# Linear attention in a hybrid backbone: chunk sums, square sums and two conditioning blocks in another order and other banks

## The chip, the cores and the metric

The kernel runs on one core of one Trainium2 chip. The metric is the device time of one launch in microseconds (us), given as the median of some runs. The engines are TensorE (PE, matrix products, with PEld for its weight loads), VectorE (DVE), ScalarE (ACT), GpSimd (POOL) and SyncE (SP, which here issues the weight transfers).

## The reference, cut to what matters

Two layers of a diffusion backbone over 256 latent tokens and 256 context tokens, width 1024, all in float32. Layer 0 mixes tokens by a gated linear attention (GLA, 4 heads, chunks of 64 tokens, forward and backward) beside a convolution; layer 1 by attention. A mixture of 16 experts follows each. Every norm is modulated by rows computed from a conditioning vector. The GLA part, for one direction:

```python
q_t = qc * jnp.exp(cum); k_t = kc * jnp.exp(-cum); k_end = kc * jnp.exp(last - cum)
att = jnp.where(mask, jnp.einsum('bhnid,bhnjd->bhnij', q_t, k_t), 0.0)
o_intra = jnp.einsum('bhnij,bhnjv->bhniv', att, vc)
u = jnp.einsum('bhnjd,bhnjv->bhndv', k_end, vc).astype(jnp.float32)
def step(s, inp):
    dec, uu = inp
    return dec[..., None] * s + uu, s
o_inter = jnp.einsum('bhnid,bhndv->bhniv', q_t, s_prev)
```

The outputs of both directions are summed, normed over the 128 values of a head, multiplied by a gate, and go with the convolution's output through one output projection:

```python
o = rms_norm(o_f + flip(o_b)) * gla_norm_g
o = o.transpose(0, 2, 1, 3).reshape(b_, t_, GLA_HEADS * GLA_DV) * jax.nn.silu(r)
out = jnp.concatenate([o, u.astype(o.dtype)], axis=-1) @ w_out
```

The conditioning rows of a layer are six slices of one product:

```python
mod = (silu_c @ ada_w[l] + ada_b[l])[:, None, :]
sh1, sc1, g1, sh2, sc2, g2 = jnp.split(mod, 6, axis=-1)
```

## The kernel before, in words

Each engine runs its own list of instructions in the order in which the code writes them; semaphores order the engines against each other. Nothing is planned at run time.

The weights come in blocks of 2 MB. `weight_stream` (L119) lists them in order of use; `ring_places` (L137) gives each one of six slots of `ring`, and SP issues them in that order (`load`, L509), each once the block six places earlier has been used (`block_used`). A few blocks go beside the ring into `xh` or `gm`. The conditioning weights of layer 1 are twelve blocks, named `("ada", 1, 0)` to `("ada", 1, 11)`; `ada_block(g, n)` (L616) multiplies block n of group g, eight matmuls with 32 stationary columns into the four partition quarters of one bank of PSUM. Group 4 is the last group: its blocks 8 to 11 are needed only for layer 1's second norm. `ada_added(g)` (L1823) adds the finished bank to the bias row on DVE, and `mod_rows(g)` (L2594) lets POOL store the row.

The GLA part works on pairs of heads, pt = 0 and 1, and for each pair on both directions d. The steps on PE, in `gla` (L841), are these. `turn_keys(pt)` transposes the end-decayed keys (L847), and ACT copies them out (`keys_taken`, L1638). `scores(pt)` makes the attention scores in four banks. DVE masks and adds them (`masked`, L2387). `chunk_sums(pt, d)` makes the eight states that a direction adds, in two banks, one for even and one for odd chunks. `inside(pt, hh)` multiplies masked scores by values (L874). DVE runs the chain of states over the chunks (`recurrence`, L2409: two copies and twelve multiply-adds). `across(pt)` multiplies queries by states, 28 matmuls of 64 columns (L888). ACT takes the outputs (`outputs_taken`, L1644), PE sums their squares over the head by a matrix of ones (`square_sums`, L835), ACT takes roots (`output_roots`, L1654), DVE inverts and scales (`normed_outputs`, L2424), and `even_out` (L937) is the output projection, whose first half goes over the convolution's four chunks of channels before it comes to the heads' four (L948).

In PSUM's eight banks, pair 0 has its scores in 0 to 3 and its outputs in 0 and 2; pair 1 has its scores in 4 to 7 and its outputs in 4 and 6. The square sums of a pair go into its own output banks.

After the projection come norm, router (`rows_and_router`, L963) and experts. In `rows_and_router` PE waits for DVE's choice of experts (`chosen`, L1014), and again for the slots (L1035); the four blocks of group 4 are multiplied ahead of these two waits, two and two. POOL then gathers the rows of the first expert from memory, and PE transposes them (L1136).

Of the kernel before, what the change touches and what calls it, by code (L numbers as in the profile page):

```python
# [118 lines left out]
def weight_stream():  # L119
# [12 lines left out]
    tail = [("eout", 0, 0), ("eout", 0, 1)] + ada(1, 8, 9, 10, 11) + moe_blocks(0)  # L132
# [30 lines left out]
def hybrid_dit(nc, A, out):  # L163
# [4 lines left out]
    with ctx:  # L168
# [169 lines left out]
        KV_BANK = (((4, 5), (1, 3)), ((1, 3), (5, 7)))  # L338
# [113 lines left out]
        ADA_BANK = (6, 2, 3, 2, 5)  # L452
# [9 lines left out]
        def ada_last(g, h):  # L462
            l, a, n = ADA_GROUPS[g]
            return at["ada", l, 2 + h if g == 0 else 2 * (a + n) - 1]
# [147 lines left out]
        def _(pe):  # L612
# [3 lines left out]
            def ada_block(g, n):  # L616
# [6 lines left out]
                if g:  # L623
                    w, s, k = flat(i).rearrange("p (c n) -> p c n", c=2), n // 4, n % 4
                    for c in range(2):
                        for q in range(4):
                            m = nc.tensor.matmul(ps[32 * q:32 * q + 32, ADA_BANK[g], :],  # L627
                                                 silu_c[:, 2 * k + c, 10 - 2 * s:42 - 2 * s], w[:, c, 512 * q:512 * q + 512],
                                                 start=n == 0 and c == 0, stop=True, skip_group_check=True)
# [205 lines left out]
            def square_sums(heads):  # L835
                for h in heads:
                    pe.wait_ge(sem("o_taken"), h + 1)
                    mm(ps[:, O_BANK[h // 2][h % 2], :], ones, (qT if h % 2 == 0 else kT)[:, h // 2, :])\
                        .then_inc(sem("o_sumsq"), 1)

            def gla():  # L841
# [20 lines left out]
                def chunk_sums(pt, d):  # L862
                    for n in range(NCH):
# [6 lines left out]
                    m.then_inc(sem("kv_sum"), 1)  # L870
# [43 lines left out]
                pe.wait_ge(sem("ketok_ready"), 4)  # L914
                chunk_sums(1, 0)
# [3 lines left out]
                chunk_sums(1, 1)  # L919
                inside(1, 1)  # L920
                across(1)
# [15 lines left out]
            def even_out():  # L937
# [3 lines left out]
                pe.wait_ge(sem("o_root"), 2)  # L941
# [21 lines left out]
            def rows_and_router(l):  # L963
# [46 lines left out]
                if l == 0:  # L1010
                    pe.wait_ge(sem("h2_act"), 2)
                    ada_block(4, 0)
                    ada_block(4, 1)
# [11 lines left out]
                else:  # L1025
# [7 lines left out]
                    ada_block(4, 2)  # L1033
# [122 lines left out]
            def down(l, e, p, i, t):  # L1156
                pe.wait_ge(arrival(i), 16 * NTH[i] + 16 * t)
                pe.wait_ge(sem("hidT_ready"), EB[l] + e + 1)
                if l == 0 and isinstance(e, int) and e == 0:
                    pe.wait_ge(sem("ada_added"), 6)  # L1160
# [277 lines left out]
        def _(act):  # L1438
# [215 lines left out]
            def output_roots(pt):  # L1654
                for hh in range(2):
                    act.wait_ge(sem("o_sumsq"), 2 * pt + hh + 1)
                    A_((qT if hh == 0 else kT)[:, pt, :], ps[:, O_BANK[pt][hh], :], ACT.Sqrt, scale=1.0 / DV, bias=eps)\
# [7 lines left out]
            def even_mixer():  # L1665
# [1145 lines left out]
```

## Time and profile before

| | us |
|---|---|
| median of 3 runs | 1047.66 (1046.27 to 1048.7) |
| the profiled execution's own time | 1039.51 |
| its span, first to last instruction | 1037.7 |
| PE busy | 949.4 (91%) |
| DVE busy | 623.6 (60%) |
| mean granted TensorE clock | 0.967 of full |

Busy times are sums over an engine's instructions; PE's matmuls overlap in its pipeline, so its busy time says when it had work and not how fast it went. The granted clock of TensorE has two levels, full (1.00, 2.4 GHz) and half (0.50, 1.2 GHz); a window that covers both shows a mean. Each float32 matmul appears as two records, so a count in the trace is twice that of the code. Times in the sections below are from the start of the span.

### The profile page before, as it was taken

The page shows a single profiled execution, that of the slowest core. Times are in us where ns is not written, and L with a number is a line of the kernel's source. Part 1 is how long each engine was busy: PE and PEld are TensorE (multiplying, and loading weights), DVE is VectorE, ACT ScalarE, POOL GpSimd, SP SyncE. Part 2 cuts the span into 40 slices and gives each one's busy share as a digit, 9 for nine tenths or more (in the row PEclk, how much of TensorE's full clock was granted, in tenths as well). Part 3 has the DMA queues.
Part 4 walks back from the last instruction along what each step waited for, and adds up shares of the span by engine and source line. Part 5 has one row for each costly group of instructions (what it writes and reads, how often), then busy time and mean ns, then how long its engine had stood idle before and what let it go on. Part 6 is the DMA issues. An engine that isn't in the chain of part 4 may idle for free.

```text
span 1037.7 us, 19786 instructions
## 1 busy us (share of the span) xinstructions
PE 949.4 (91%) x7940; PEld 575.5 (55%) x7940; DVE 623.6 (60%) x1516; ACT 178.0 (17%) x339; POOL 114.9 (11%) x176
## 2 busy tenths in 40 slices
PE   3999999989998799999999997997997999988896
PEld 1443433457445588988988973443646455543442
DVE  1200799787456586676675636467435977775553
ACT  2100022353024010000000013225413000000001
POOL 7100100102300100000001132100101100000000
PEclk9999999997999699999999998999997999999999
DMA  9999876442826999999999959646034989999994
GB/s 332 398 392 369 327 268 218 164 163 84 250 91 243 383 357 362 403 417 405 391 402 407 424 181 356 245 167 237 6 104 180 346 339 400 399 385 412 417 429 171
DMA packets 51354, 311.94 MB, mean 301 GB/s; under 512 B 7096, under 2 KB 8888, under 8 KB 33632
## 3 DMA queue, kind: packets, MB, share of 16 engines
q1 hardware_dynamic: 36752, 277.88, 68.2%
q0 software_dynamic: 9376, 21.19, 6.7%
q10 hardware_dynamic: 5168, 12.06, 3.1%
q8 instruction: 41, 0.67, 0.3%
q14 instruction: 17, 0.14, 0.0%
HBM read 300.52 MB, written 17.25 MB: 306 GB/s over the span
## 4 chain that ended last, share of the span: by engine, by line
PE 69%; DMA 16%; DVE 9%; issue 2%; SPq 2%; ACT 2%; POOL 0%; ACTq 0%; DVEq 0%; POOLq 0%
PE ps L614 46%; PE ps L1054 9%; DMA ring<-in_moe_w_gate 8%; PE ps L948 3%; PE ps L627 3%; DMA ring<-in_moe_w_down 2%; DMA ring<-in_ada_w 2%; PE ps L1097 2%; PE ps L1175 2%; SPq L515 2%; DMA y_rows<-ar 1%; PE ps L888 1%; DMA xh<-y_rows,sm 1%; DMA ar<-h_rows,sm 1%; PE ps L1418 1%
## 5 line engine op out<-in xcount | busy, mean ns | idle before, releaser
L614 PE MATMUL ps<-ring,ar 128*32 128x384 f32 (+6 forms) x3872 | 479.8, 466 | 17.9 <-DMA ring<-in_moe_w_gate 13.7
L614 PEld LDWEIGHTS ps<-ring,ar 128*32 128x32 f32 (+2 forms) x3872 | 198.7, 121 | 145.3 <-issue 87.1
L1054 PE MATMUL ps<-ring,ar 128*32 128x128 f32 x1488 | 167.8, 275 | 0.0
L1054 PEld LDWEIGHTS ps<-ring,ar 128*32 128x32 f32 x1488 | 163.7, 111 | 2.7
L2171 DVE STREAM_TRANSPOSE ar<-ar 32x256 f32<-32x256 f32 x304 | 132.2, 435 | 5.0 <-issue 0.6
L614 PE MATMUL ps<-xh,ring 128*128 128x512 f32 x256 | 114.9, 603 | 0.7 <-DMA ring<-in_even_w_in 0.7
L2214 DVE TENSOR_TENSOR ar<-ar,ps 128x384 f32<-128x384 f32 (+2 forms) x33 | 15.9, 482 | 132.1 <-PE ps L1054 68.1
L614 PE MATMUL ps<-ring,xh 128*128 128x512 f32 x192 | 85.9, 604 | 1.9 <-ACT xh L1478 1.6
L614 PEld LDWEIGHTS ps<-xh,ring 128*128 128x128 f32 x256 | 48.3, 192 | 64.2 <-issue 62.9
L2343 DVE SCALAR_TENSOR_TENSOR ar<-ar,cpar 128x512 f32<-128x512 f32 x120 | 79.6, 742 | 0.0
L1530 ACT ACTIVATE ar<-ps 128x384 f32<-128x384 f32 (+2 forms) x33 | 14.3, 433 | 289.7 <-PE ps L614 205.7
L614 PEld LDWEIGHTS ps<-ring,xh 128*128 128x128 f32 x192 | 36.5, 193 | 48.6 <-issue 45.6
L2201 DVE STREAM_TRANSPOSE ar<-ar 32x64 f32<-32x64 f32 x256 | 60.5, 236 | 4.5
L2193 DVE STREAM_TRANSPOSE ar<-ar 32x128 f32<-32x128 f32 x144 | 59.5, 413 | 2.9
L1097 PE MATMUL ps<-ring,ar 128*32 128x256 f32 x256 | 57.9, 379 | 0.0
L2650 POOL COPY sm<-sm 96x1 int32 (+3 forms) x32 | 6.0, 187 | 342.4 <-DVE ar L2171 318.3
L627 PE MATMUL ps<-ring,silu_c 128*32 128x512 f32 x320 | 39.9, 619 | 0.0
L2311 DVE TENSOR_TENSOR ar<-ps,gm 128x512 f32<-128x512 f32 x12 | 8.3, 689 | 51.7 <-PE ps L614 39.8
L1097 PEld LDWEIGHTS ps<-ring,ar 128*32 128x32 f32 x256 | 28.0, 110 | 18.1
L614 PE MATMUL ps<-ar 128*128 128x512 f32 (+3 forms) x112 | 33.3, 464 | 4.6 <-ACT ar L1767 2.4
L1535 ACT ACTIVATE ar<-ps 128x512 f32<-128x512 f32 x16 | 9.6, 598 | 149.3 <-PE ps L614 149.3
L2654 POOL DMA_INDIRECT ar<-h_rows,sm x32 | 31.2, 976 | 27.9 <-POOL sm L2650 26.8
(371 smaller groups left out, 908.9 us busy)
## 6 DMA issues: line engine op xcount, KB each, us to landing
ring<-in_moe_w_gate SPq DMA_DIRECT2D x31, 2048.0 KB, 17.1
ring<-in_moe_w_up SPq DMA_DIRECT2D x30, 2048.0 KB, 15.6
ring<-in_moe_w_down SPq DMA_DIRECT2D x30, 2048.0 KB, 19.1
ring<-in_ada_w SPq DMA_DIRECT2D x24, 2048.0 KB, 10.5
ring<-in_even_w_in SPq DMA_DIRECT2D x5, 2048.0 KB, 14.0
y_rows<-ar POOLq DMA_DIRECT2D x17, 384.0 KB, 10.5
ring<-in_odd_w_in SPq DMA_DIRECT2D x3, 2048.0 KB, 18.1
y_rows<-ar ACTq DMA_DIRECT2D x16, 288.0 KB, 8.9
```

Source lines behind the costliest of these rows:

```text
L515: sp.dma_start(wide, s).then_inc(arrival(i), 16)
L614: return nc.tensor.matmul(o, l, r, start=start, stop=stop)
L627: m = nc.tensor.matmul(ps[32 * q:32 * q + 32, ADA_BANK[g], :], silu_c[:, 2 * k + c, 10 - 2 * s:42 - 2 * s], w[:, c, 512 * q:512 * q + 512] ...
L948: m = nc.tensor.matmul(ps[:, j, :], mix[:, c, j * P:(j + 1) * P], blk(i)[:, c, :], start=(c == 4), stop=(c == 3), skip_group_check=True)
L1054: m = nc.tensor.matmul(ps[96:128, bank, g * P:(g + 1) * P], xgT[:, p, c, 32 * g:32 * g + 32], w[:, c, 3 * P:HID], start=c == 0 and g == 0, ...
L1097: nc.tensor.matmul(ps[96:128, 5, 256 * g:256 * g + 256], tokens(g, c), w[:, c, 768:D], start=c == 0 and g == 0, stop=c == HC - 1 and g == ...
L1175: m = nc.tensor.matmul(acc(j, h), mixw[64 * h:64 * h + 64, p, j * P:(j + 1) * P], yb[64 * h:64 * h + 64, p, 0:512], start=False, stop=True ...
L2171: m = V.transpose(xgT[32 * q:32 * q + 32, p, :, slots], xg[slots, p, :].rearrange("s (c q i) -> s q c i", c=KC, q=4)[:, q, :, :])
L2193: V.transpose(hidT[32 * q:32 * q + 32, p, :, 32 * r:32 * r + 32], cols[:, q, :, :])
L2201: m = V.transpose(hidT[32 * q:32 * q + 32, p, 0:2, 32 * r:32 * r + 32], cols[:, q, :, :])
L2343: V.scalar_tensor_tensor(acc[n], u_in[:, n, :, bass.ds(t, 256)], cpar[:, n, bass.ds(t, 1)], acc[n], ALU.mult, ALU.add).then_inc(sem("conv_ ...
L2654: G.indirect_dma_start(xg[0:CAP[l], p, :], None, h2_rows, bass.IndirectOffsetOnAxis(ap=idxc[0:CAP[l], p:p + 1], axis=0), bounds_check=NT * ...
```

## The change

The tail of the weight stream is in another order: blocks 8 and 9 of layer 1's conditioning weights stand ahead of the output projection's two blocks, 10 and 11 behind them.

```diff
-    tail = [("eout", 0, 0), ("eout", 0, 1)] + ada(1, 8, 9, 10, 11) + moe_blocks(0)
+    tail = ada(1, 8, 9) + [("eout", 0, 0), ("eout", 0, 1)] + ada(1, 10, 11) + moe_blocks(0)
```

Banks: the backward chunk sums of pair 1 go into 0 and 2, and the square sums get banks of their own (`SQ_BANK`). Blocks 8 and 9 are summed in bank 6, 10 and 11 in bank 5.

```diff
-        KV_BANK = (((4, 5), (1, 3)), ((1, 3), (5, 7)))
+        KV_BANK, SQ_BANK = (((4, 5), (1, 3)), ((1, 3), (0, 2))), ((5, 7), (4, 6))
...
-        ADA_BANK = (6, 2, 3, 2, 5)
+        ADA_BANK = (6, 2, 3, 2, 6)
+        LATE_BANK = 5
```

PE's order in `gla`, where `chunk_sums` can now make some chunks only:

```diff
-                chunk_sums(0, 0)
+                chunk_sums(0, 0).then_inc(sem("kv_sum"), 1)
                 pe.wait_ge(sem("att_masked"), 2)
+                chunk_sums(0, 1, range(0, NCH, 2))
                 inside(0, 0)
                 pe.wait_ge(sem("att_masked"), 4)
-                chunk_sums(0, 1)
+                chunk_sums(0, 1, range(1, NCH, 2)).then_inc(sem("kv_sum"), 1)
                 inside(0, 1)
                 pe.wait_ge(sem("qk_exp"), 8)
                 pe.wait_ge(sem("ke_diff"), 4)
+                ada_block(4, 0)
+                ada_block(4, 1)
                 across(0)
                 turn_keys(1)
+                pe.wait_ge(sem("ada_added"), 6)
                 scores(1)
-                square_sums((0, 1))
                 pe.wait_ge(sem("ketok_ready"), 4)
-                chunk_sums(1, 0)
+                chunk_sums(1, 0).then_inc(sem("kv_sum"), 1)
+                pe.wait_ge(sem("o_taken"), 2)
+                chunk_sums(1, 1).then_inc(sem("kv_sum"), 1)
                 pe.wait_ge(sem("att_masked"), 6)
                 inside(1, 0)
                 pe.wait_ge(sem("att_masked"), 8)
-                chunk_sums(1, 1)
                 inside(1, 1)
+                square_sums((0, 1))
                 across(1)
```

In `even_out` the wait for pair 0's roots goes. In `rows_and_router` one block stands ahead of each of the two waits instead of two.

```diff
-                pe.wait_ge(sem("o_root"), 2)
...
                     pe.wait_ge(sem("h2_act"), 2)
-                    ada_block(4, 0)
-                    ada_block(4, 1)
+                    ada_block(4, 2)
...
                     pe.wait_ge(sem("h2_act"), NT)
-                    ada_block(4, 2)
                     ada_block(4, 3)
```

ACT copies pair 1's keys before it takes pair 0's outputs. DVE adds blocks 8 and 9 between `decayed(1)` and `masked(1)`, and 10 and 11 where the whole group was added before:

```diff
+                keys_taken(1)
                 outputs_taken(0)
-                keys_taken(1)
...
                 decayed(1)
+                ada_added(4)
                 masked(1)
...
+            def late_added():
+                dve.wait_ge(sem("block_used"), at["ada", 1, 11] + 1)
+                V.tensor_tensor(modrow_of(4), modrow_of(4), ps[:, LATE_BANK, :], ALU.add).then_inc(sem("ada_added"), 1)
...
-                    ada_added(4)
+                    late_added()
```

PE in the first head pair, before (`gm` holds this pair's queries and keys, `ar` the values and states; 64x128 is a chunk sum):

```order
L614 MATMUL ps<-gm 128x128 x16
L614 MATMUL ps<-ar,gm 64x128 x16
L874 MATMUL ps<-gm,ar 128x128 x4
L614 MATMUL ps<-ar,gm 64x128 x16
L874 MATMUL ps<-gm,ar 128x128 x4
L888 MATMUL ps<-gm,ar 128x64 x28
```

And PE at the same place now:

```order
L615 MATMUL ps<-gm 128x128 x16
L615 MATMUL ps<-ar,gm 64x128 x24
L876 MATMUL ps<-gm,ar 128x128 x4
L615 MATMUL ps<-ar,gm 64x128 x8
L876 MATMUL ps<-gm,ar 128x128 x4
L628 MATMUL ps<-ring,silu_c 32x512 x16
L890 MATMUL ps<-gm,ar 128x64 x28
```

Eight chunk sums moved ahead of the first `inside`, and the sixteen matmuls of two conditioning blocks stand ahead of `across(0)`.

PE in the second head pair, before (`xh` holds its queries and keys; `ar,cst 128x512` is a square sum):

```order
L847 MATMUL ps<-cst,xh 128x128 x8
L614 MATMUL ps<-xh 128x128 x16
L614 MATMUL ps<-ar,cst 128x512 x2
L614 MATMUL ps<-ar,xh 64x128 x16
L874 MATMUL ps<-xh,ar 128x128 x4
L614 MATMUL ps<-ar,xh 64x128 x16
L874 MATMUL ps<-xh,ar 128x128 x4
L888 MATMUL ps<-xh,ar 128x64 x28
```

And PE there now:

```order
L849 MATMUL ps<-cst,xh 128x128 x8
L615 MATMUL ps<-xh 128x128 x16
L615 MATMUL ps<-ar,xh 64x128 x32
L876 MATMUL ps<-xh,ar 128x128 x8
L615 MATMUL ps<-ar,cst 128x512 x2
L890 MATMUL ps<-xh,ar 128x64 x28
```

All 32 chunk sums now stand ahead of both `inside` steps, and the square sums of pair 0 behind them.

SP's transfers around the output projection's weights, before:

```order
L515 DMA ring<-in_even_w_in 128x8x512
L515 DMA ring<-in_even_w_out 128x8x512 x2
L515 DMA ring<-in_ada_w 128x2x2048 x4
L515 DMA ring<-in_moe_w_gate 128x4096
L515 DMA ring<-in_moe_w_up 128x4096
```

And SP there now:

```order
L516 DMA ring<-in_even_w_in 128x8x512
L516 DMA ring<-in_ada_w 128x2x2048 x2
L516 DMA ring<-in_even_w_out 128x8x512 x2
L516 DMA ring<-in_ada_w 128x2x2048 x2
L516 DMA ring<-in_moe_w_gate 128x4096
L516 DMA ring<-in_moe_w_up 128x4096
```

Two conditioning blocks moved ahead of the projection's two; the expert blocks behind them take the slots in this new order of release.

## Rows read from the trace of the kernel before

**Rows 1.** Timeline of PE (start, duration in us, line, tiles, records; idle before).

```profile
219.36 1.04 PE L847 MATMUL ps<-cst,gm 128*128 128x128 f32 x8
220.32 2.06 PE L614 MATMUL ps<-gm 64*128 64x128 f32 x32
...
226.06 1.10 PE L614 MATMUL ps<-ar,gm 64*64 64x128 f32 x32 [0.94 <-DVE gm L2406]
227.09 1.16 PE L874 MATMUL ps<-gm,ar 128*128 128x128 f32 x8
230.84 6.03 PE L888 MATMUL ps<-gm,ar 64*128 64x64 f32 x56 [2.59 <-DVE ar L2421]
236.80 1.97 PE L847 MATMUL ps<-cst,xh 128*128 128x128 f32 x8
...
241.92 1.98 PE L614 MATMUL ps<-ar,cst 128*128 128x512 f32 x4
...
250.57 5.36 PE L888 MATMUL ps<-xh,ar 64*128 64x64 f32 x56 [2.42 <-DVE ar L2421]
255.86 4.95 PE L948 MATMUL ps<-ring,ar 128*128 128x512 f32 x8
...
262.36 24.20 PE L948 MATMUL ps<-ring,ar 128*128 128x512 f32 x56
```

**Rows 2.** Timeline of DVE in the same stretch.

```profile
227.11 0.48 DVE L2418 COPY ar<-ps 128x128 f32<-128x128 f32 x2
227.51 3.17 DVE L2421 SCALAR_TENSOR_TENSOR ar<-ar,ps 128x128 f32<-128x128 f32 x12
...
233.02 1.28 DVE L2385 TENSOR_TENSOR xh<-xh,ar 128x512 f32<-128x512 f32 x2
...
242.04 0.73 DVE L2398 COPY_PREDICATED xh<-cst,ps 128x512 f32<-128x512 uint32 x1 [0.50 <-PE ps L614]
...
244.91 0.69 DVE L2406 TENSOR_TENSOR xh<-xh 128x512 f32<-128x512 f32 x1
...
247.13 0.29 DVE L2418 COPY ar<-ps 128x128 f32<-128x128 f32 x1 [1.33 <-PE ps L614]
...
250.44 3.34 DVE L2429 RECIPROCAL ar<-ar 128x512 f32<-128x512 f32 x1
```

**Rows 3.** Windows of 1 us (busy time and records by engine, granted clock, DMA).

```profile
229.00:230.00 1.00, 0.00 (x0) 0.00 (x0) 1.00 (x5) 0.99 (x3) 0.00 (x0) 1.00 0.00 0
...
231.00:232.00 1.00, 1.00 (x14) 1.00 (x13) 1.00 (x3) 1.00 (x2) 0.00 (x0) 0.55 0.00 0
...
242.00:243.00 1.00, 1.00 (x3) 0.52 (x4) 0.92 (x2) 0.00 (x0) 0.00 (x0) 1.00 0.13 45
```

**Rows 4.** Timeline of ACT: start of the outputs' and of the keys' copies.

```profile
236.84 0.60 ACT L1648 ACTIVATE ar<-ps 128x512 f32<-128x512 f32 x1 [2.65 <-PE ps L888]
...
239.29 1.08 ACT L1641 ACTIVATE xh<-ps 128x512 f32<-128x512 f32 x2
```

**Rows 5.** Timeline of PE in the router.

```profile
327.70 3.64 PE L627 MATMUL ps<-ring,silu_c 128*32 128x512 f32 x32
331.50 1.29 PE L1018 MATMUL ps<-ar,cst 128*128 128x80 f32 x10 [0.16 <-DVE ar L1988]
```

**Rows 6.** Chain of waits: the first gather (start, us, what).

```profile
339.14 10.39 DMA ar<-h_rows,sm
```

**Rows 7.** DMA issues near 286, 360 and 400 us (size, us to landing).

```profile
ring<-in_moe_w_gate SPq DMA_DIRECT2D x1, 2048.0 KB, 7.9
...
ring<-in_moe_w_down SPq DMA_DIRECT2D x1, 2048.0 KB, 11.3
...
ring<-in_moe_w_down SPq DMA_DIRECT2D x1, 2048.0 KB, 9.7
```

**Rows 8.** Waits of PE from 550 to 570 us (total, times, longest).

```profile
PE ps L614 <- DMA ring<-in_moe_w_gate: 1.9, 1, 1.9
PE ps L614 <- DMA ring<-in_moe_w_down: 0.3, 1, 0.3
```

More of the change, by code:

```diff
@@ L463, in ada_last @@
             l, a, n = ADA_GROUPS[g]
-            return at["ada", l, 2 + h if g == 0 else 2 * (a + n) - 1]
+            return at["ada", l, 2 + h if g == 0 else 9 if g == 4 else 2 * (a + n) - 1]
         def xn_of(k):
@@ L626, in ada_block @@
                         for q in range(4):
-                            m = nc.tensor.matmul(ps[32 * q:32 * q + 32, ADA_BANK[g], :],
+                            m = nc.tensor.matmul(ps[32 * q:32 * q + 32, LATE_BANK if g == 4 and n >= 2 else ADA_BANK[g], :],
                                                  silu_c[:, 2 * k + c, 10 - 2 * s:42 - 2 * s], w[:, c, 512 * q:512 * q + 512],
-                                                 start=n == 0 and c == 0, stop=True, skip_group_check=True)
+                                                 start=n == (2 if g == 4 and n >= 2 else 0) and c == 0, stop=True,
+                                                 skip_group_check=True)
                     m.then_inc(sem("block_used"), 1)
@@ L837, in square_sums @@
                     pe.wait_ge(sem("o_taken"), h + 1)
-                    mm(ps[:, O_BANK[h // 2][h % 2], :], ones, (qT if h % 2 == 0 else kT)[:, h // 2, :])\
+                    mm(ps[:, SQ_BANK[h // 2][h % 2], :], ones, (qT if h % 2 == 0 else kT)[:, h // 2, :])\
                         .then_inc(sem("o_sumsq"), 1)
@@ L860, in scores, with chunk_sums @@
                         m.then_inc(sem("att"), 1)
-                def chunk_sums(pt, d):
-                    for n in range(NCH):
+                def chunk_sums(pt, d, chunks=range(NCH)):
+                    for n in chunks:
                         lo = CHUNK * (n % 2)
@@ L869, in chunk_sums @@
                                    v_tok[lo:lo + 64, n // 2, (2 * pt + hh) * P:(2 * pt + hh + 1) * P])
-                    m.then_inc(sem("kv_sum"), 1)
+                    return m
                 def inside(pt, hh):
@@ L1159, in down @@
                 if l == 0 and isinstance(e, int) and e == 0:
-                    pe.wait_ge(sem("ada_added"), 6)
+                    pe.wait_ge(sem("ada_added"), 7)
                 if not (isinstance(e, int) and e == 0) and not narrow(l, e):
@@ L1656, in output_roots @@
                     act.wait_ge(sem("o_sumsq"), 2 * pt + hh + 1)
-                    A_((qT if hh == 0 else kT)[:, pt, :], ps[:, O_BANK[pt][hh], :], ACT.Sqrt, scale=1.0 / DV, bias=eps)\
+                    A_((qT if hh == 0 else kT)[:, pt, :], ps[:, SQ_BANK[pt][hh], :], ACT.Sqrt, scale=1.0 / DV, bias=eps)\
                         .then_inc(sem("o_root"), 1)
@@ L2596, in mod_rows @@
                 l, a, n = ADA_GROUPS[g]
-                pool.wait_ge(sem("ada_added"), g + 2)
+                pool.wait_ge(sem("ada_added"), 7 if g == 4 else g + 2)
                 for s in range(n // 2):
```

## The prediction

> **What bounds the kernel now.** I read the page first (PE busy 91% of the span), then the chain of waits, then the timelines of PE, DVE and ACT where the diff works, the granted clock in windows of 1 us, and last the DMA issues and PE's waits for them in the expert loop. Around the change PE and DVE take turns. PE stands 2.59 us until DVE's first chain of states is done (230.84), and 2.42 us at the second (250.57) [rows 1]; DVE's second chain in turn starts late, because its last copy waits 1.33 us for PE's chunk sums [rows 2]. The clock is worth as much as the waits. After the first idle stretch it drops from 1.00 at 229 us to 0.55 at 231 and is full again only at 242 [rows 3]. `across` alone, though PE was busy all through its 6.03 us, did not bring it back; the transposes that follow took 1.97 us against 1.04 for the same eight records at full clock [rows 1]. The same happens again at 250.57: `across(1)` takes 5.36 us, and the first eight records of the output projection 4.95, where 56 of them take 24.20, that is 0.432 each or 3.46 for eight [rows 1].
>
> **First pair.** The two copies of the state chain start at 227.11, right behind other DVE work, and the twelve steps end at 230.68 [rows 2]. The chunk sums issued earlier therefore bring the chain at most 0.1 us; I take 0. PE: the masked scores let it go at 226.06; half of the 1.10 us of chunk sums is left, then 1.16 of `inside`, so it is free at 227.75 instead of 228.25 [rows 1]. Two conditioning blocks follow, 3.64 us for 32 records at full clock [rows 5]: done at 231.4. `across(0)` starts 0.55 us later than its 230.84; that is what the overhang costs. In return PE was never idle ahead of it. At full clock `across` takes half of 6.03, so 3.0 (bounds: 6.03, as measured at half clock, and 3.0, half of it; I take 3.0, since the transposes' 1.97 and 1.04 show the same halving). It ends at 234.4 and not at 236.8.
>
> **Second pair.** The keys are ready at 234.3 [rows 2], so the transposes start at 234.4 and end at 235.4. The new wait, ahead of the scores, is for DVE's addition of the row: one 128x512 instruction of some 0.7 us behind 234.3, done at 235.0, so hidden; behind this wait stand the scores, and DVE's masking waits for them. Scores take 2.06 us [rows 1]: done at 237.5. Before, they ended at 241.92. DVE then needs from its last wait for scores (242.04) to the second masked sum (244.91 plus 0.69) 3.56 us [rows 2], so masking ends at 241.1, not 245.6. Now the order of chunk sums counts: both sets are done by 237.5 plus 2.2 = 239.7, if their banks are free. The first waits for ACT's keys, now copied first: 1.08 us [rows 4] from about 235.0, done by 236.1. The second waits for pair 0's outputs, which ACT leaves within 2.4 us of its start on them (before from 236.84, with the keys started at 239.29 [rows 4]), so at 238.5, under the first set of sums. So the state chain starts when DVE is free, at 241.1, and takes 0.48 plus 3.17: it ends at 244.7 where it ended at 250.5. In it lie the last `inside` (1.16) and the square sums (four records of 0.432, 1.7): 241.2 to 244.1. Moved there, the square sums cost nothing; without that cover they would cost 1.7. `across(1)` runs from 244.9 to 247.9. Before, the projection started at 255.86: 7.9 us earlier.
>
> **Projection.** 64 records of products and four of square sums at 0.432 are 29.4 us, against 30.7 from 255.86 to the end of the last row at 286.56 [rows 1]. It ends at 277.3: 9.2 us earlier. Two things could be late next. DVE's four heads of the norm (3.34 us of reciprocal plus two passes of about 0.7, some 4.85 each with the links) run from 244.7 to 264.1; the last head is multiplied from about 273.9. And the projection's weights, now issued behind two other blocks, into slots released tens of microseconds before; a block lands in 7.9 us [rows 7]. The wait for roots that the diff removes was over long before: 0. I take 0.4 off for handovers: 8.8 us.
>
> **Router.** The 3.64 us of blocks lay under DVE's choice; PE was idle only 0.16 us after them [rows 5]. Taking one block away gives nothing: DVE sets that wait. Taken the other way, PE now stands some 1.9 us there and the clock may drop earlier; the five small matmuls of 1.29 us could take 2.6, of which 0.6 are under a DVE instruction. Bounds 0 and 0.7 slower; I take 0. The second addition to the row on DVE is one for one. The first gather takes 10.39 us from issue to landing [rows 6], beside running weight transfers. One fewer of these is queued ahead of it, yet the next two start at about the same time. Bounds 0 and 1.5 faster (the block ahead of it landed in 7.9 when alone); I take 0.
>
> **Expert loop.** Two slots are released 90 us earlier, in a stretch where DMA rests, so the first two expert blocks come in early, and the third to fifth each move up. But a landing time of 11.3 us at 360 us falls to 9.7 at 400 [rows 7] though blocks are used at the same pace: the queue drains there by itself, and a block alone takes 7.9. At most 9.7 less 7.9, 1.8 us of advance, survives to the long loop. There PE waits 1.9 and 0.3 us [rows 8], 2.2 together. I take 1.8 of them; bounds 0 and 2.2.
>
> The sum is 8.8 + 0 + 0 + 1.8 = 10.6 us. From the profiled execution's 1039.51 (span 1037.7) this gives 1028.9. That execution was 8.15 us under the median of the runs, 1047.66, and nothing in its trace says where the others lose it; I apply the same difference to the median: 1037.0.
>
> **A rule that speaks against it.** The sum lets `across` go twice as fast at full clock. Its 56 records take 108 ns each at half clock; scores, with the same 64x128 weights loaded for each record, take 2.06 us for 32 at full clock, 64 ns each [rows 1]. By the Trainium skill, TensorE: Matmul & The Clock Gate (LDWEIGHTS), a weight load takes its number of columns over 1.2 GHz, 107 ns for 128, and no faster clock is given for it; by that rule `across` would stay at 6.0 us. The scores' 64 ns disagree, and I go by them.
>
> **Rivals.** First, the clock falls between `across(0)` and the scores. For it: `across` did not raise it. Against it: the fall in the rows came behind 2.59 us without work [rows 1, 3]. Transposes (+0.95) and scores (+2.06) at half clock make masking 3.0 us later, and all behind it: 7.6 gained, 1040.1. If it falls behind `across(1)` instead, the first eight records cost 1.5 more: 1038.5, inside the forecast's own range.
>
> Second, weight loads and not the clock set `across`. For it: 108 ns a record, steady; against it: the scores. Each `across` is then 3.0 longer; the projection starts at 254.0 and ends at 283.4, 3.2 earlier, and with 1.8 it is 5.0: 1042.7. This is the case of the page's rule above.
>
> Third, the advance in the ring is kept in full: 2.2 us of waits go, and the loop's last stores find a queue that is emptier by as much, so the gathers behind them come 2.2 earlier again: 13.2, 1034.5. Against it stands the drain at 400.
>
> Fourth, no change: the blocks fill PE's idle time, but the experts start when their data come, by something in gather or weights that doesn't move with the projection. For it only that the gather takes 10.39 us [rows 6]; against it, all transfers there are released by PE or DVE. 1047.7.
>
> Fifth, slower: the clock falls in the blocks' stretch and stays at half until the projection. It decides at 231.4. Then `across` 6.03, transposes 1.97, scores 4.1 and chunk sums 4.4 put the chunk sums' end at 247.9, the states' at 251.6; `inside` and square sums at half take PE to about 256, and `across(1)` to 262, 6 us later than before, with 2 more in the projection's start and 1.8 gained in the loop: 6 us slower, 1053.7. Against it: before the change, the same transposes and scores stand where the clock came back, by 242 [rows 3].
>
> **Numbers.** Forecast 49%, first rival 20%, second 8%, third 12%, fourth 6%, fifth 5%. The forecast's own range is 1035.5 to 1039. For 8 in 10, with the first and third rival, the bounds above, and the spread of the runs (1046.27 to 1048.7): 1033.0 to 1042.5; the second lies at its edge. Runs of this kernel can't tell a change under about 0.2%, 2.1 us. Faster 0.89, same 0.06, slower 0.05.
>
> **What would show it.** In the profile after: no idle time on PE ahead of the first `across`, and 3.0 us for it at a clock of 1.00; scores of pair 1 done near 237.5; DVE's second chain without a wait for PE and from about 241; the projection from about 248 to 277; less than 1 us of PE waiting for weights between 530 and 570 (shifted by 9). I am wrong if `across(0)` still takes over 5 us, if DVE waits for chunk sums at its second chain, or if the expert stage starts less than 6 us earlier.

## The result, and the profile after

The changed kernel took 1030.11 us in the median of four runs (1028.4 to 1031.51) against 1048.18 of the kernel before beside it (1046.27 to 1049.07): ratio 0.9845, 95% interval 0.9814 to 0.9875. Two later comparisons of the same pair (with e5 and e11), on two chips, gave 0.9853 (0.9813 to 0.9893) and 0.9838 (0.9813 to 0.9863). By the medians the change is worth 16 to 18 us, where 10.6 were forecast and the range ended at 14.7: 1030.11 us against a forecast of 1037.0 and a range of 1033.0 to 1042.5. The direction was right, the size was outside the range.

PE's timeline after, of the stretch of [rows 1] (start, duration in us, line, tiles, records; idle before):

```profile
227.06 1.16 PE L876 MATMUL ps<-gm,ar 128*128 128x128 f32 x8
228.15 3.64 PE L628 MATMUL ps<-ring,silu_c 128*32 128x512 f32 x32
231.72 3.34 PE L890 MATMUL ps<-gm,ar 64*128 64x64 f32 x56
235.00 1.09 PE L849 MATMUL ps<-cst,xh 128*128 128x128 f32 x8
236.02 2.06 PE L615 MATMUL ps<-xh 64*128 64x128 f32 x32
238.00 2.20 PE L615 MATMUL ps<-ar,xh 64*64 64x128 f32 x64
...
245.23 3.74 PE L890 MATMUL ps<-xh,ar 64*128 64x64 f32 x56 [0.62 <-DVE ar L2429]
248.90 4.94 PE L954 MATMUL ps<-ring,ar 128*128 128x512 f32 x8
```

The 2.59 us of idle time ahead of the first `across` (L890) are gone; it takes 3.34 us instead of 6.03, and of the 2.42 us of idle time ahead of the second 0.62 are left. The output projection starts at 248.90, not 255.86. DVE's timeline, against [rows 2]:

```profile
241.60 0.48 DVE L2426 COPY ar<-ps 128x128 f32<-128x128 f32 x2
242.00 3.18 DVE L2429 SCALAR_TENSOR_TENSOR ar<-ar,ps 128x128 f32<-128x128 f32 x12
```

The second chain of states begins right behind the masking: no wait for chunk sums stands there. The clock, in windows of 1 us, against [rows 3]:

```profile
229.00:230.00 1.00, 1.00 (x16) 0.36 (x12) 1.00 (x5) 0.99 (x3) 0.00 (x0) 1.00 0.00 0
231.00:232.00 1.00, 1.00 (x13) 0.28 (x6) 1.00 (x3) 1.00 (x3) 0.00 (x0) 1.00 1.46 262
...
248.00:249.00 1.00, 1.00 (x13) 0.88 (x9) 0.96 (x2) 0.01 (x1) 0.00 (x0) 0.51 0.73 250
```

The granted clock stands in the column behind the five busy times: 1.00 at 231 us where it was 0.55. It falls only at 248, as `across(1)` ends, and is full again by 252.

The larger surprise is 90 us further on. PE's timeline in the router, against [rows 5]:

```profile
320.74 1.92 PE L628 MATMUL ps<-ring,silu_c 128*32 128x512 f32 x16
324.54 1.29 PE L1023 MATMUL ps<-ar,cst 128*128 128x80 f32 x10 [1.88 <-DVE ar L1996]
...
334.68 1.97 PE L615 MATMUL ps<-ar 128*128 128x32 f32 x16 [1.14 <-DVE ar L2068]
336.62 1.39 PE L1140 MATMUL ps<-cst,ar 96*128 96x96 f32 x8
338.80 0.86 PE L615 MATMUL ps<-ring,ar 128*32 128x384 f32 x3 [0.78 <-DVE ar L2173]
```

L1140 transposes the rows of the first gather and has nothing to wait for. Before, the same matmuls began at 349.66, behind 6.1 us of waiting:

```profile
PE ps L1136 <- DMA ar<-h_rows,sm: 6.1, 1, 6.1
```

The ranks (L1023) are 7.0 us earlier, the first expert product 13.2. The first gather, issued at 332.19, against the 10.39 us of [rows 6] (issues, us to landing):

```profile
ar<-h_rows,sm POOLq DMA_INDIRECT x1, 4.3
```

SP's issues show what else was running. After:

```profile
322.72 0.33 SPq L516 DMA_DIRECT2D ring<-in_moe_w_down  x1
333.61 0.33 SPq L516 DMA_DIRECT2D ring<-in_moe_w_gate  x1
333.98 0.43 SPq L516 DMA_DIRECT2D xh<-in_moe_w_up  x1
```

Before:

```profile
329.69 0.33 SPq L515 DMA_DIRECT2D ring<-in_moe_w_gate  x1
331.41 0.33 SPq L515 DMA_DIRECT2D ring<-in_moe_w_up  x1
338.28 0.33 SPq L515 DMA_DIRECT2D ring<-in_moe_w_down  x1
341.12 0.33 SPq L515 DMA_DIRECT2D ring<-in_moe_w_gate  x1
341.49 0.43 SPq L515 DMA_DIRECT2D xh<-in_moe_w_up  x1
```

G, U and D stand for an expert's gate, up and down weights, 0 for the first expert. Before, U1 (331.41, 13.1 us to landing) and D0 are running when the gather is issued at 339.14; G2 and U2 follow 2 us behind it. After, U1 has long landed, D0 was sent 16 us earlier and landed by about 331 (an estimate from the 8.2 us that it took in the second profile of this kernel), and no weight transfer runs at 332.19; G2 and U2 follow 1.4 us behind. In the loop, PE's waits for weights are what they were in [rows 8]:

```profile
PE ps L615 <- DMA ring<-in_moe_w_gate: 1.9, 1, 1.9
PE ps L615 <- DMA ring<-in_moe_w_down: 0.3, 1, 0.3
```

### The profile page after: what moved, and what is told of

It reads as the page before. It is cut to its first block, busy times and chain, and to the rows that moved or that the text cites. A ratio compares the mean times of both kernels' runs of the same rounds, so it can differ in the third digit from the quotient of the medians.

```text
span 1029.7 us, 19788 instructions
## 1 busy us (share of the span) xinstructions
PE 955.8 (93%) x7940; PEld 575.5 (56%) x7940; DVE 624.2 (61%) x1517; ACT 177.6 (17%) x339; POOL 115.4 (11%) x176
## 4 chain that ended last, share of the span: by engine, by line
PE 73%; DMA 13%; DVE 8%; issue 2%; SPq 2%; ACT 2%; ACTq 0%; DVEq 0%
PE ps L615 48%; DMA ring<-in_moe_w_gate 11%; PE ps L1058 10%; PE ps L628 3%; PE ps L954 3%; PE ps L1101 2%; DMA ring<-in_ada_w 2%; PE ps L1179 2%; SPq L516 2%; PE ps L1422 1%; PE ps L890 1%; DVE xh L1870 1%; PE ps L1214 0%; DVE ss L2540 0%; ACT xh L1482 0%
## 5 line engine op out<-in xcount | busy, mean ns | idle before, releaser
L615 PEld LDWEIGHTS ps<-ring,ar 128*32 128x32 f32 (+2 forms) x3872 | 200.9, 121 | 150.8 <-issue 90.7
L2222 DVE TENSOR_TENSOR ar<-ar,ps 128x384 f32<-128x384 f32 (+2 forms) x33 | 15.9, 482 | 134.7 <-PE ps L615 69.0
## 6 DMA issues: line engine op xcount, KB each, us to landing
ring<-in_moe_w_up SPq DMA_DIRECT2D x30, 2048.0 KB, 14.3
ring<-in_even_w_in SPq DMA_DIRECT2D x5, 2048.0 KB, 10.9
ring<-in_odd_w_in SPq DMA_DIRECT2D x3, 2048.0 KB, 18.1
```

Source lines behind the costliest of these rows:

```text
L615: return nc.tensor.matmul(o, l, r, start=start, stop=stop)
```

## Where the time went, over eight executions

One profile of each kernel is not enough here: the shown one of before was 8 us faster than the median of its timed runs, and one stretch after the expert loop (the last narrow expert) differs by 7 us between executions of one kernel. So the kernels were profiled again under new labels, before five times and after three times in all. Lengths of the stretches in us; "keys" is the start of the first head pair's transposes, "last narrow expert" the time from SP's issue of the next layer's first weights to that of its output weights:

| stretch | before: shown, e1, e12, e13, e14 | mean | after: shown, e5, e11 | mean | gained |
|---|---|---|---|---|---|
| keys to projection | 36.5, 34.5, 35.3, 34.6, 36.7 | 35.5 | 29.6, 29.2, 29.2 | 29.3 | 6.2 |
| projection to ranks | 75.6, 76.1, 76.9, 76.0, 76.8 | 76.3 | 75.6, 74.4, 74.4 | 74.8 | 1.5 |
| ranks to first expert product | 20.5, 22.5, 23.8, 17.2, 18.0 | 20.4 | 14.3, 14.8, 14.4 | 14.5 | 5.9 |
| from there to the last narrow expert | 271.0, 269.9, 269.0, 271.2, 271.7 | 270.6 | 268.7, 271.0, 268.8 | 269.5 | 1.1 |
| last narrow expert | 16.5, 16.5, 23.5, 22.1, 23.5 | 20.4 | 23.3, 16.7, 21.4 | 20.5 | -0.1 |
| rest | 398.3, 400.8, 399.4, 401.0, 399.8 | 399.9 | 398.9, 400.8, 400.4 | 400.0 | -0.2 |

The gains sum to 14.4 us (mean spans 1042.8 and 1028.4). The forecast had 8.8 for the first two rows, 0 for the third, 1.8 for the fourth. The third row is a mean over unlike executions: before, PE waited 6.1, 7.4, 8.4, 2.6 and 3.2 us for the first gather. In two of the five POOL could not even issue it in time, because the last store of the rows that it reads (`h_rows<-ar`, 512 KB) was late: that store took 9.0 us in e1 and 10.4 in e12, and the gather went out 8.6 and 10.2 us behind the ranks instead of 7.6. That is 0.7 us of the mean of 5.9.

## The experiments

**e1, the kernel before under a new label.** No edit.

> The kernel before, unchanged. The profile on which the prediction rested was of an execution of 1039.5 us, while the timed ones take 1046 to 1049. Theory: that execution was the odd one, and a usual one loses some 8 us in the second half (behind layer 0's experts), as the changed kernel does there; then this profile's span is 1045 to 1047, its first half agrees with the one shown within 0.5 us (first expert product at 352), and the difference lies behind 590 us. Rival: the difference lies in the expert loop, where a slower transfer rate makes PE wait more than the 2.2 us seen; then the wait for ring blocks between 500 and 590 us is over 6 us.

1042.37 us (1039.74 to 1047.02), ratio 1.001 (0.9981 to 1.0039). Neither theory of the expectation holds for this execution: its span is 1040.2, its last narrow expert takes 16.5 us as in the shown one, and PE's waits for weights in the loop are 2.2 us. Its first `across` took 4.01 us, where the shown execution has 6.03. The clock, in windows of 1 us:

```profile
231.00:232.00 1.00, 0.60 (x11) 0.63 (x12) 1.00 (x3) 1.00 (x3) 0.00 (x0) 1.00 0.00 0
233.00:234.00 1.00, 1.00 (x22) 1.00 (x21) 1.00 (x3) 1.00 (x3) 0.00 (x0) 0.94 0.00 0
234.00:235.00 1.00, 1.00 (x14) 1.00 (x12) 0.87 (x2) 0.75 (x2) 0.00 (x0) 0.50 0.00 0
```

Here the clock falls near 233.9 (worked out from the mean of 0.94 in its window), when PE has already run 2.5 us of `across` at 1.00; in the shown execution it falls near 231.1 [rows 3], 0.3 us behind the start of `across`. The idle stretch ahead is 2.59 us in both. What differs between executions is when, behind it, the clock falls.

**e2, the new order without the early blocks.** Blocks 8 to 11 back at their old place in the stream, in PE's order and in DVE's; chunk sums, square sums and ACT's order new. The cut below is against the kernel after.

```diff
-                ada_block(4, 0)
-                ada_block(4, 1)
                 across(0)
```

> Only the order and banks of chunk and square sums, and ACT's order; the conditioning blocks stay in the router, the weight stream as before. Theory: of the 7.0 us that the projection starts and ends earlier in the changed kernel, the earlier chunk sums give 1.5 to 3.5 (the second state chain no longer waits 1.33 us for sums, square sums leave the path), and the clock still falls ahead of the first across, so that this takes 6.0 us. First expert product 2 to 4 us earlier, the first gather still lands in about 10 us. Total 2 to 4 us faster than before. Rival: the order is what gives the 7 us, and the blocks only fill time; then 7 us.

1035.62 us (1032.82 to 1041.4), ratio 0.9932 (0.9898 to 0.9966). PE's timeline:

```profile
230.98 6.24 PE L890 MATMUL ps<-gm,ar 64*128 64x64 f32 x56 [2.59 <-DVE ar L2428]
237.15 1.97 PE L849 MATMUL ps<-cst,xh 128*128 128x128 f32 x8
239.05 2.76 PE L615 MATMUL ps<-xh 64*128 64x128 f32 x32
...
248.97 3.34 PE L890 MATMUL ps<-xh,ar 64*128 64x64 f32 x56 [0.61 <-DVE ar L2428]
252.24 3.70 PE L951 MATMUL ps<-ring,ar 128*128 128x512 f32 x8
```

The clock falls in the first pair as before, but the second pair's wait shrinks to 0.61 us and the clock holds to the projection. The order's worth in this stage is all in the second pair: keys to projection 32.7 us, 2.8 under the mean of before. From there to the ranks it is 74.4, 1.9 under it. The first gather took 7.7 us here, not the 10 expected, and PE waited 2.5 for it; U1 was running beside it all the same, so the waits spread widely. The total, 5.1 us under the 1040.72 of before beside it, is above the 2 to 4 expected.

**e3, the early blocks with the old order.** Old banks of chunk and square sums, their old places, old order on ACT; weight stream and banks of the blocks as in the kernel after. The cut below is against the kernel before.

```diff
+                ada_block(4, 0)
+                ada_block(4, 1)
                 across(0)
```

> Only the blocks: two of the last group multiplied ahead of the first across, with the weight stream that this needs; order and banks of chunk and square sums as before. Theory: the clock stays full through the first across and the scores (across 3.3 us), worth 3 to 5 us up to the projection, and the first gather lands in 4 to 5 us instead of 10.4, worth 5 to 6 more: 9 to 11 us faster in all in the first half. Rival: gather time has nothing to do with the blocks; then the first expert product is only 3 to 5 us earlier.

1033.09 us (1028.16 to 1036.3), ratio 0.9883 (0.9838 to 0.9929). PE's timeline:

```profile
234.21 3.34 PE L890 MATMUL ps<-gm,ar 64*128 64x64 f32 x56
...
249.14 6.20 PE L890 MATMUL ps<-xh,ar 64*128 64x64 f32 x56 [2.42 <-DVE ar L2428]
255.27 5.76 PE L953 MATMUL ps<-ring,ar 128*128 128x512 f32 x8
```

The mirror of e2: the first pair is quick, the second has its 2.42 us of wait and its half clock back. Keys to projection is 33.5, 2.1 under the mean of before; yet the median is 7.6 us under that of before, against 5.1 for e2, though the two intervals overlap. The rest lies behind the ranks: the first gather took 4.5 us, PE did not wait for it at all, and ranks to first product took 13.9.

**e4, the kernel before with the gather ahead of weights.** SP waits for the first gather to land before it issues D0, G2 and U2.

```diff
+                if l == 0:
+                    sp.wait_ge(sem("xg_in0"), 16)
                 expert_load("d", 0)
```

> The kernel before, with SP waiting for the landing of the first gather before it issues the first expert's down block and what follows it. Theory: the first gather takes 10.4 us only because weight transfers run beside it; with none issued after about 332 us it lands in 4 to 6 us, and the first expert product starts 5 to 6 us earlier (346). Rival: the gather's time is its own; then it stays at about 10 us and the first product at 352. What comes in total is open: the ring starts later, so up to 5 us of it can be given back in the loop.

1042.64 us (1038.58 to 1045.1), ratio 1.0001 (0.9976 to 1.0026): nothing. The gather landed in 4.0 us and PE's wait for it fell to 2.3; ranks to first product took 16.8, against 20.4 in the mean of before. The first product came at 348.62, not at the 346 expected, because the gather itself was issued late, 11.1 us behind the ranks and not 7.6. The last store of its rows had gone out 0.5 us behind G1 and took 10.9 us. POOL:

```profile
341.55 0.34 POOL L2652 COPY sm<-sm 96x1 int32<-96x1 int32 x1 [7.90 <-DMA h_rows<-ar]
```

And the weights held back are missing later. PE's waits for weights, 400 to 600 us:

```profile
PE ps L616 <- DMA ring<-in_moe_w_gate: 6.2, 4, 2.2
PE ps L616 <- DMA ring<-in_moe_w_down: 0.2, 1, 0.2
```

6.4 us for 2.3 in the same stretch of the shown execution, and the stretch from first product to last narrow expert took 275.5 us, 4.9 over the mean of before: the gain is given back in the loop. D0, G2 and U2 were all held back, so e4 does not say which of them costs it.

**e5, the kernel after under a new label.** No edit.

> The changed kernel, unchanged, beside many runs of the kernel before on the same chip. Theory: executions of the kernel before lie anywhere from 1037 to 1049 us, and the four it was first compared with were late ones; beside more of them the gain is 10 to 13 us (ratio 0.987 to 0.990), not 17. Rival: the changed kernel is 16 us faster on every chip; ratio 0.9845 again. And in this profile: if the 6 us in which PE stood without a releaser in the last expert of layer 0 are part of the change, they are there again (second layer's input weights to output weights 23 us); if they belong to one execution, it is 16.5 us as in the four other kernels.

1027.38 us (1025.17 to 1035.32) beside 1043.64 of before, ratio 0.9853 (0.9813 to 0.9893). The gain is 16.3 us, nearer to the rival than to the theory (10 to 13), though the interval reaches into the theory's range; the last narrow expert took 16.7 us, so its 23.3 in the first profile are no part of the change. PE's timeline at the projection:

```profile
245.97 3.34 PE L890 MATMUL ps<-xh,ar 64*128 64x64 f32 x56 [0.61 <-DVE ar L2429]
249.24 3.70 PE L954 MATMUL ps<-ring,ar 128*128 128x512 f32 x8
```

Here the clock did not fall behind `across(1)`; eight records take 3.70, not 4.94. The same 3.70 stands in all eight later profiles with this order.

**e6, the kernel after with its weights late.** SP holds back the first five expert blocks (G0, U0, G1, U1, D0) to about where the kernel before sent them; PE, DVE and ACT unchanged. `LATER` names for each of them a later block that must have been used (cut):

```diff
-                    sp.wait_ge(sem("block_used"), NEED[i])
+                    sp.wait_ge(sem("block_used"), LATER.get(stream[i], NEED[i]))
```

> The changed kernel with the first five expert blocks held back on SP to where the kernel before issued them: the first two behind the projection's two halves, two more behind the block ahead of the choice, the fifth behind the last conditioning block. The work on PE, ACT and DVE is the changed kernel's. Theory: the stage up to the projection keeps its 7 us, but the gather runs beside weight transfers again and lands in 9 to 10 us instead of 4.3: first expert product 4.5 to 6 us later than in the changed kernel, total 4 to 6 us slower than it. Rival (my prediction's): the gather takes the same time either way and the advance in the ring is worth 1 to 2 us; then total 1 to 2 us slower.

1033.43 us (1028.23 to 1034.0), ratio 0.9889 (0.9855 to 0.9923). With the same engine work up to the ranks (29.2 and 74.4 us, as in e5) the wait is back. PE's waits, then the landing of the first gather:

```profile
PE ps L1143 <- DMA ar<-h_rows,sm: 6.5, 1, 6.5
```

```profile
ar<-h_rows,sm POOLq DMA_INDIRECT x1, 11.1
```

Ranks to first product: 21.2, against 14.8 in e5. These 6.4 us are what the early weights bring, and the median moved by 6.0. The rival, a gather that takes the same time either way, is out.

**e7, both late blocks ahead of the choice.** `ada_block(4, 3)` one wait earlier, so its slot is free earlier, and G2 and U2 go out at 323.9, beside the gather.

```diff
                     ada_block(4, 2)
+                    ada_block(4, 3)
                 pe.wait_ge(sem("chosen"), l + 1)
```

> The changed kernel with both of the last conditioning blocks ahead of the choice of experts, so the slots of both are free 9 us earlier and weight transfers (the third expert's gate and up) run beside the gather. Theory: gather back at 8 to 10 us, first expert product 4 to 6 us later; the ring is further ahead in return, which gives back at most the 2.2 us of waits: total 2 to 5 us slower than the changed kernel. Rival: early weights are good in any case; then it is no slower and the waits for ring blocks in layer 0 are gone.

1032.05 us (1029.35 to 1033.66), ratio 0.9888 (0.9857 to 0.9919): 4.7 us behind e5 by the medians. PE's waits there:

```profile
PE ps L615 <- DVE ar L2068: 5.9, 1, 5.9
PE ps L1140 <- DMA ar<-h_rows,sm: 4.5, 1, 4.5
```

Weights earlier still make the kernel slower, since they are still running when the gather is issued (10.5 us). But PE also stood 5.9 us where it now has no block to multiply, so e7 alone doesn't say which of the two costs it.

**e8, the new order with a filler in place of the blocks.** e2 with sixteen matmuls of the blocks' shape that feed nothing, ahead of `across(0)`; no slot is released by them.

```diff
+                for f in range(16):
+                    nc.tensor.matmul(ps[32 * (f % 4):32 * (f % 4) + 32, 6, :], silu_c[:, f // 4, 10:42], cst[:, 0:512],
+                                     start=True, stop=True, skip_group_check=True)
                 across(0)
```

> The kernel with the order and banks alone (conditioning blocks in the router, weight stream as before), with 16 matmuls added that read constants into a free bank and whose result nobody uses, ahead of the first across. They take the place and the time of the two conditioning blocks (3.6 us), without any weight slot being freed. Theory: the clock stays at full through across, transposes and scores as in the changed kernel (across 3.3 us), and the projection starts 3 us earlier than with the order alone, within 0.5 us of the changed kernel; but the gather still lands in 9 to 10 us. Total 2 to 4 us faster than the order alone, 4 to 6 us slower than the changed kernel. Rival: it is the earlier slots and not the clock; then nothing is gained on the order alone.

1032.44 us (1029.5 to 1035.77), ratio 0.9892 (0.9859 to 0.9925). Keys to projection 29.2, as in e5 and e11: for the clock sixteen matmuls whose result nobody uses do what the blocks do. But PE waits 5.2 us for the gather again (10.3 us to landing, U1 running, D0 sent 1.5 us behind it), and the total is 5.1 us behind e5. This separates the change's two gifts: clock and waits in this stage come from filled idle time, the rest from slots that are free early.

**e9, e7 with the gather guarded.** Both blocks early, and SP waits for the first gather before G2 (D0 stays ahead of it).

```diff
                 if l == 0:
+                    sp.wait_ge(sem("xg_in0"), 16)
                     expert_load("g", 2)
```

> The kernel after with both late conditioning blocks ahead of the choice, as in e7, but SP waits for the first gather before it issues G2 and U2. Theory (the gather is slow when weight transfers run beside it): the gather lands in some 4.3 us again, PE doesn't wait for it, the first expert product starts within 1 us of 338.5, and the time is within 2 us of e5's 1027.4. Rival (e7 lost its 4.7 us through DVE's slots being late or through the half clock, not through the gather): the first product stays at about 344 and the time at about 1032.

1031.47 us (1030.14 to 1032.75), ratio 0.9844 (0.9822 to 0.9866), beside 1029.9 for the kernel after (e11, same chip). The first gather:

```profile
ar<-h_rows,sm POOLq DMA_INDIRECT x1, 4.1
```

Ranks to first product 15.9, against 20.6 in e7 (on another chip, with the same 29.2 and 74.4 us up to the ranks), first product at 339.56. As the guard changes nothing on PE or DVE ahead of the gather, the 4.6 us between them are the gather beside G2 and U2. The 1.4 us more than in the kernel after (14.5) are at the slot matmuls, which behind 4.74 us without work took 3.59 us and not 1.97. Two of the expected figures were missed: the first product by 0.1 us, and the total, named as within 2 us of e5's 1027.4, by 2 (it is 4.1 off); against e11 of the same chip it is 1.6.

**e10, the kernel after with the same guard.**

> The kernel after, with SP waiting for the first gather before it issues G2 and U2 (D0 stays ahead). Theory: the transfers are out of the gather's way already, so the guard changes little: gather some 4.3 us, G2 issued 1 to 3 us later than 332.5, the loop's waits for weights 2.7 plus at most 1, total within 1.5 us of the kernel after (1027.4). Rival (the cushion of the ring is what counts, as in the kernel before with the gather first, whose loop waits grew from 2.2 to 6.3): the loop's waits grow by 3 or more and the total is 1030 or later.

1032.43 us (1029.8 to 1035.86), ratio 0.9854 (0.983 to 0.9877), against 0.9838 (0.9813 to 0.9863) of e11: the medians are 2.5 us apart, the intervals overlap, so the two are not told apart. The total is 5 us over the 1027.4 named and in the rival's range (1030 or later), but e11, on the same chip, is at 1029.9 without the guard. G2 went out at 337.05, and the loop's waits were 1.5 us, so the rival's 3 more didn't come. No gain from the guard is seen.

**e11, the kernel after once more.**

> The kernel after once more, as the comparison for the two runs beside it and a third profile of it: total 1027 to 1030, gather about 4.3 us. Whether PE stalls in the last narrow expert as in the first profile (some 6.8 us between 592 and 607): if that is a property of the kernel, it is there again; if of the one execution, it is not, and the last narrow expert takes 16.5 us as in the others.

1029.9 us (1029.27 to 1035.56) beside 1047.8 of before, ratio 0.9838. PE again stalled in the last narrow expert (21.4 us).

**e12, e13 and e14, the kernel before three more times,** on one chip, to find where its slower executions lose their time.

> The kernel before, one more profile. Its executions spread from 1037 to 1051 us, and both profiles so far are of 1039.5 and 1042.0. Theory A: an execution near 1047 loses 4 to 7 us in the last narrow expert (PE idle with no releaser between some 610 and 625 us, odd_in to odd_out issue 20.9 or more instead of 16.5), as four of the five latest profiles of the kernel after do. Theory B: it loses them at a half clock around the states and the projection or in the router (projection's start later than 256.5, or its first product later than 353). Theory C: spread over the expert loops. An execution under 1043 should show none of it.

> The same kernel and theories as in the run beside it: A, odd_in to odd_out issue of 20.9 or more in an execution near 1047; B, the projection's start later than 256.5 us or the first expert product later than 353; C, spread over the expert loops. What both executions show alike belongs to the chip they run on, what differs to the execution.

> The same kernel and theories a third time: A, odd_in to odd_out issue of 20.9 or more in an execution near 1047; B, the projection's start later than 256.5 us or the first expert product later than 353; C, spread over the expert loops.

1050.01, 1043.71 and 1047.67 us. All three have the long last narrow expert: 23.5, 22.1 and 23.5 us, against 16.5 in the shown execution and e1. PE's timeline there in e12:

```profile
611.88 0.44 PE L614 MATMUL ps<-ring,ar 128*32 128x128 f32 x5 [0.34 <-issue]
612.64 0.43 PE L614 MATMUL ps<-ring,ar 128*32 128x128 f32 x5 [0.32 <-issue]
613.39 0.44 PE L614 MATMUL ps<-ring,ar 128*32 128x128 f32 x6 [0.33 <-issue]
```

and in the first profile of the kernel after, the same pattern:

```profile
595.34 0.43 PE L615 MATMUL ps<-ring,ar 128*32 128x128 f32 x5 [0.31 <-issue]
596.09 0.44 PE L615 MATMUL ps<-ring,ar 128*32 128x128 f32 x5 [0.33 <-issue]
```

Five matmuls, then a pause that nothing in the trace releases. Theory A holds for the last narrow expert, but not alone: e13, at 1043.71, has its 22.1 us too, and is as quick as it is because it waits only 2.6 us for the first gather. In the fourteen profiles whose chip is known the stall goes with the chip: none of the eight profiles on two chips has it (16.5 to 17.7 us), all six on two others do (20.9 to 23.5), whichever kernel runs. B adds a little in e12 only (first product at 356.25); e13 and e14 have it at 347.67 and 350.85, earlier than the shown 351.96.

## Why the prediction was right in direction and wrong in size

**The stage: right, 7 to 8 us of 8.8.** The chain ran as forecast: no idle time ahead of the first `across`, clock at 1.00, scores done at 238.1 (237.5 forecast), masking at 241.6 (241.1), states at 245.2 (244.7) without a wait for PE, square sums hidden, projection at 248.90 (247.9). Of the 1.0 us between, 0.3 is there when `across(1)` starts (245.23, 244.9 forecast) and the rest comes from `across(1)` itself, 3.7 us for 3.0. Halving 6.03 was slightly too good: 3.34 is what the 56 records take at 1.00, 6.24 at 0.50 (e2), a factor of 1.87, and the shown 6.03 began at full clock. In the profile after, the clock fell behind `across(1)` and eight records cost 1.24 us more, the variant named under the first rival (1.5). In the seven later profiles with this order and a filled first pair it held. In the means, keys to ranks is 7.7 us.

**The rule that spoke against it: wrong here.** The 56 records of `across` take 60 ns each at a granted clock of 1.00 and, from the 6.03 and 6.24 us, 108 to 111 at 0.50. The Trainium skill, TensorE: Matmul & The Clock Gate (LDWEIGHTS), gives columns over 1.2 GHz, that is 107 ns for 128, and names no clock level; in these runs a record takes about that long only at 0.50. The second rival is excluded by this. The first rival's main form (the fall between `across(0)` and the scores) came in none of the profiles with filled idle time.

**The first gather: the step that failed.** The prediction took 0, with a bound of 1.5, because of the weight transfers running beside the gather "one fewer of these is queued ahead of it, yet the next two start at about the same time". Measured, for the stretch from ranks to first product: 5.9 us in the means (6.2 between the two shown profiles), of which 0.7 is the late store of the rows. The second half of that sentence came true: G2 goes out 2.0 us behind the gather before and 1.4 after, and it does no harm there. The first half miscounted: with two slots released at 230, every expert block behind moves up by one or two releases, and no weight transfer is left running when the gather is issued. In the shown execution of before these were two, U1 and D0. U1 alone does as much: in e1, e13 and e14 D0 was sent 0.5 to 1.5 us behind the gather, which took 11.5, 7.6 and 8.5 us all the same. Why it takes 7.6 in one execution and 11.5 in another with the same transfers beside it is not known. The bound failed with the count. It was taken from the 7.9 us of a 2 MB weight block, for a transfer of another kind; no row showed the same gather without a weight transfer running, and with nothing near it the bound had to be PE's whole wait for it, 6.1 us. e6, e7 with e9, and e8 show the mechanism from three sides: 6.4, 4.6 and 5.6 us come back when weights run beside the gather again. e4 shows that it isn't free for the taking in the kernel before.

**The wait for the choice: right.** PE stood 1.88 us ahead of the ranks (1.9 forecast), and the ranks kept their 1.29 us. The clock fell only behind them, at no cost that shows: from the ranks to the slot matmuls it is 10.1 us in both shown profiles.

**The loop: 1.8 forecast, at most 1.1.** Waits for weights were 2.2 before and 2.2 after. The stretch's mean is 1.1 us shorter, less than executions of one kernel differ (2.7). The drain that was cited against the third rival takes nearly the whole advance: D1 goes out at 346.60 and not at 360.08, 13.5 us earlier, where the first product is 13.2 earlier.

**From the profile to the median: the step held, by luck.** The shown profile was 8.15 us under the median of 1047.66. e14, an execution of 1047.67, spends 7.1 us more in the last narrow expert than the shown one. Both kernels pay this on such a chip, so applying the same difference to both came out right, but no row of the prediction said so; that the timed runs of before lost their time there is likely and not shown, since they have no profile. The stall misleads whoever compares the two shown profiles: the spans 1037.7 and 1029.7 differ by 8.0, and the stall, which only the second has, hides 6.9 more.

**What stays open.** The profiles give 14.4 us, the timed medians 16.3 to 18.1; the intervals of the three ratios reach down to 13.1, 11.2 and 14.4 us, so no further mechanism is needed, but none is excluded. Why two chips pause after the loop and two don't wasn't tried. By the Trainium skill, Runtime: NRT & Kernel Launch (Instruction fetch mechanics), a taken branch whose target is not in the two pages of instructions at hand must have its page fetched before the engine goes on. PE's loop over experts ends shortly before, but no run here shows the fetch. No version tried beats the kernel after.

## What to carry to other kernels

Filling an idle stretch of PE with work that is due later brought three things here: the work's own time, the clock for what follows, and earlier slots for the loads behind; price each by itself. When a release moves up, follow every transfer behind it to the next small transfer that an engine waits for, and ask which transfers stop running beside it: the wait for that one, in whole, is the bound. And before subtracting two profiles, compare stretches that the change can't touch: 7 us here went with the chip.

## What the runs showed of the hardware

The first gather (96 rows, indirect) landed in 4.0 to 4.7 us in the six profiles in which no weight transfer was running when it was issued (after, e3, e5, e9, e11) or one with 2 us left (e4). It took 7.6 to 11.5 in the nine others whose trace has it (before, e1, e2, e6, e7, e8, e12 to e14), in which one or two were running. G2, sent 1.2 to 1.5 us behind it in after, e3, e5 and e11, did not slow it. The last store of its rows (512 KB) shows the like: sent 0.2 us ahead of G1 it took 3.4 to 4.0 us (before, e13, e14), sent 0.03 to 0.5 us behind G1 9.0 to 10.9 (e1, e12, e4).

Executions of one kernel differ in when the clock falls behind the same idle stretch (2.59 us on PE in all five of before). By the means of the 1 us windows it fell 0.6 us ahead of the start of the first `across` in e14 and 0.3 behind it in the shown execution, but 1.6 behind it in e12 and 2.4 to 2.5 in e13 and e1. `across` took 6.24 and 6.03 us in the first two, 4.82, 4.12 and 4.01 in the others. It took 3.34 in all nine profiles in which work filled the idle time of the first pair.
